# A 2 by 2 block scheme with seven block products for the gate and up products of a streaming encoder's feed-forward network

## The reference, cut to what matters

```
x = x + token_mix(rmsnorm(x, norm_mix), ...)          # attention, pooling, latent attention, convolution
h = rmsnorm(x, norm_ffn)                              # 640 tokens x 1024
x = x + (silu(h @ w_ff_gate) * (h @ w_ff_up)) @ w_ff_down
y = rmsnorm(x, norm_final)                            # after the second layer
```

## Time and profile before

| what | value |
|---|---|
| median of 3 runs | 2607.0 us (2605.19, 2607.0, 2620.18) |
| profiled execution | 2600.69 us, span 2598.9 us |
| TensorE busy, matmuls | 2454.0 us (94%), 15714 |
| mean granted TensorE clock | 0.969 of full |
| VectorE busy | 1063.2 us (41%) |
| ScalarE busy | 567.0 us (22%) |
| GpSimd busy | 1189.8 us (46%) |
| DMA | 186.01 MB, mean 72 GB/s |

### The profile page before, as it was taken

One profiled execution on the slowest core, in us unless ns is written; L12 is line 12 of the kernel. 1 busy time (PEld: TensorE's weight loads), 2 busy tenths in 40 slices (PEclk: granted clock), 3 DMA queues, 4 the chain that ended last, 5 costly groups with the idle time before them and its releaser, 6 DMA issues.

```text
span 2598.9 us, 44801 instructions
## 1 busy us (share of the span) xinstructions
PE 2454.0 (94%) x15714; PEld 2302.1 (89%) x15714; DVE 1063.2 (41%) x1940; ACT 567.0 (22%) x1080; POOL 1189.8 (46%) x1364
## 2 busy tenths in 40 slices
PE   6997999999999999999899889999999999999996
PEld 5996997777899999999899789977778999999996
DVE  6976253333236331232379643433322363303323
ACT  2014233333312210010111232323332121100100
POOL 3542554222366555655445335522214665555552
PEclk9998998999999999999899999989987999999998
DMA  5341121001132222222324312201001322222222
GB/s 170 126 120 33 62 67 52 29 25 37 37 123 74 75 66 73 84 78 67 122 70 134 92 45 70 65 25 37 25 25 49 122 74 73 69 78 81 73 65 73
DMA packets 73084, 186.01 MB, mean 72 GB/s; under 512 B 20381, under 2 KB 23549, under 8 KB 71934
## 3 DMA queue, kind: packets, MB, share of 16 engines
q1 hardware_dynamic: 55230, 161.54, 19.7%
q10 hardware_dynamic: 17728, 22.78, 2.7%
HBM read 171.72 MB, written 14.14 MB: 72 GB/s over the span
## 4 chain that ended last, share of the span: by engine, by line
PE 88%; DVE 4%; issue 3%; ACT 2%; ACTq 2%; DMA 1%; SPq 0%; DVEq 0%
PE gemm L466 75%; PE side L705 1%; PE side L723 1%; PE side L691 1%; PE side L707 1%; DVE rstd L1210 1%; PE side L708 1%; PE side L699 1%; PE side L715 1%; DVE h_lo L1215 1%; PE side L677 1%; PE side L609 1%; DVE softmax_stats L1476 0%; ACTq L1054 0%; ACT square L1098 0%
## 5 line engine op out<-in xcount | busy, mean ns | idle before, releaser
L431 POOL CAST w_hi<-w_raw 128x384 fp32r<-128x384 f32 (+3 forms) x680 | 397.2, 584 | 1320.9 <-PE gemm L466 1294.9
L433 POOL TENSOR_TENSOR w_lo<-w_raw,w_hi 128x384 fp32r<-128x384 f32 (+3 forms) x680 | 795.7, 1170 | 54.4
L466 PE MATMUL gemm<-h_hi,w_hi 128*128 128x320 f32 x3136 | 737.6, 317 | 21.7 <-DVE h_lo L1215 15.7
L466 PE MATMUL gemm<-h_lo,w_hi 128*128 128x320 f32 x3136 | 719.4, 311 | 0.0
L466 PE MATMUL gemm<-h_hi,w_lo 128*128 128x320 f32 x3136 | 718.9, 311 | 0.0
L466 PEld LDWEIGHTS gemm<-h_hi,w_hi 128*128 128x128 f32 x3136 | 525.4, 189 | 41.2 <-issue 33.7
L466 PEld LDWEIGHTS gemm<-h_lo,w_hi 128*128 128x128 f32 x3136 | 528.9, 189 | 0.0
L466 PEld LDWEIGHTS gemm<-h_hi,w_lo 128*128 128x128 f32 x3136 | 528.8, 189 | 0.0
L1292 DVE SCALAR_TENSOR_TENSOR side<-conv_prompt,vec,side 128x512 f32<-128x512 f32 x232 | 173.5, 748 | 0.0
L1534 DVE TENSOR_TENSOR x<-gemm,x 128x320 f32<-128x320 f32 x96 | 42.6, 486 | 302.3 <-PE gemm L466 302.3
L466 PE MATMUL gemm<-f_lo,w_hi 128*128 128x320 f32 x704 | 160.5, 309 | 0.0
(11 more groups left out here) (222 smaller groups left out, 2673.1 us busy)
## 6 DMA issues: line engine op xcount, KB each, us to landing
w_raw<-in_ws_gate SPq DMA_DIRECT2D x64, 512.0 KB, 3.4
w_raw<-in_ws_in SPq DMA_DIRECT2D x44, 512.0 KB, 3.4
w_raw<-in_ws_fg SPq DMA_DIRECT2D x44, 512.0 KB, 3.3
w_raw<-in_ws_fu SPq DMA_DIRECT2D x44, 512.0 KB, 3.3
w_raw<-in_ws_proj SPq DMA_DIRECT2D x64, 256.0 KB, 2.6
w_raw<-in_ws_d SPq DMA_DIRECT2D x32, 384.0 KB, 3.0
w_raw<-in_ws_d SPq DMA_DIRECT2D x32, 320.0 KB, 2.8
w_raw<-in_ws_out SPq DMA_DIRECT2D x16, 512.0 KB, 3.3
```

What stands on the lines that cost most here:

```text
L431: eng.tensor_copy(w_hi[s][:, cols], w_raw[s][:, cols]).then_inc(w_high.sem, 1)
L433: eng.tensor_tensor(w_lo[s][:, cols], w_raw[s][:, cols], w_hi[s][:, cols].bitcast(F32), ALU.subtract).then_inc(w_split.sem, 1)
L466: mm = eng.matmul(dst[:, hf, 0:HALF], w, r[:, k, cols], start=first and k == 0 and part == 0, stop=last and k == kk - 1 and part == 2)
```

## The change

**Seven products.** The gate tiles j and j+1, as a 1024 x 256 block of weights against 640 tokens, are seen as a 2 by 2 by 2 block product: weight blocks b11, b12 (first 4 weight tiles of tile j and of j+1) and b21, b22 (the last 4), activation blocks by token half and by half of the 1024 features. Plainly this is 8 block products of 12 matmuls (4 weight tiles, 3 parts, 320 tokens). The new code forms four sums of weights (T1 to T4) and four of activations (S1 to S4) and needs seven block products. One such group of seven is a *quad*; gate and up have one each per pair of tiles, 10 pairs and so 20 quads per layer. The first pair (tiles 0 and 1) stays plain: 4 units.

**Where it accumulates.** The five regions QX, QV (G[0]), QY, QW (G[1]) and QZ (bank 6) are 128x320. ACT copies a finished product from one region into the next one, where a later product is added on top, and into u2 and u4 in SBUF; DVE makes the last two sums.

**Activation blocks.** They need `rstd` inside, so DVE makes them after the norm: `act_block` (4 instructions of 128x320), `act_sum` (128x1280), ACT rounds with `act_high`, DVE `act_low`, once per layer, beside units 0 to 3 (listed at `gate_out(0)`). h_hi and h_lo are overwritten by them; the plain h of the feed-forward half is hu_hi, hu_lo.

**Weights.** Four raw buffers of 128x1024, and a ring of 5 hi/lo operands of 128x512. ACT now does all rounding (`cast`), POOL subtracts for plain operands, DVE for the sums of weights (`sum_low`) and makes the sums themselves (`weight_sums`).

**Chunks** are now 8, 8 and 6 tiles, so down units have 8, 8 and 6 weight tiles, 8 units in each chunk. **Both layers and all feed-forward tiles are written out** in Python instead of `Fori`. SP loads the small mixing weights of the second layer only after the last feed-forward product of the first, since the ring lies over them.

The diff, cut to its core (blank lines left out):

```diff
-K6, K5 = 6, 5
 CUT = 3
 UW = DM
+HW = UW // 2
+RING = 5
 BIG = float(2.0 ** 100)
 
...
+    def quad():
+        a = len(loads)
+        b = a + 1
+        quads.append(len(ops))
+        add(a, 0, HW)
+        first = plain
+        add(b, 1, HW, F_SUM3)
+        add(a, 0, HW, F_SUM2)
+        add(b, 0, HW)
+        add(a, 1, HW, F_SUM1)
+        loads.append((UW, first, sums))
+        add(b, 0, HW, F_SUM4)
+        add(b, 1, HW)
+        loads.append((UW, plain, sums))
...
         m_lo, o = sb("m_lo", [P, KT, T], F32R, o)
 
...
+        hu_hi, o = sb("hu_hi", [P, KT, T], F32R, o)
+        hu_lo, o = sb("hu_lo", [P, KT, T], F32R, o)
+        assert o == m_at
+        ah, al, af = [None] * 7, [None] * 7, [None] * 7
+        for n in range(4, 7):
+            ah[n], o = sb(f"act_hi{n}", [P, 4, HALF], F32R, o)
+            af[n], _ = sb(f"act{n}", [P, 4, HALF], F32, o)
...
+        f_lo01, o = sb("f_lo", [P, 2, T], F32R, o)
...
 
         relb, _ = sb("rel_bias_sb", [NBUCKET, NH], F32, R)
         hot, _ = sb("bucket_hot", [NBUCKET, RELW], F32, R + 64)
         relv, _ = sb("rel_values", [NH, RELW], F32, R + 64 + RELW * 4)
 
         G = [ctx.enter_context(nc.psum_tensor(f"gemm{s}", [P, 2, 512], F32)) for s in range(2)]
+        QX, QV, QY, QW = G[0][:, 0, 0:HALF], G[0][:, 1, 0:HALF], G[1][:, 0, 0:HALF], G[1][:, 1, 0:HALF]
...
+                for r, (width, _, _) in enumerate(FF_LOADS):
+                    if r < 2:
+                        eng.wait_ge(w_split.sem, w_split.at(l, 2 * UNITS - 2 + 2 * r))
+                    elif r < 4:
+                        eng.wait_ge(unit_done.sem, unit_done.at(l, UNITS - 1))
+                    else:
+                        _, plain, sums = FF_LOADS[r - 4]
+                        eng.wait_ge(lo_plain.sem, lo_plain.at(l, plain))
+                        if sums:
+                            eng.wait_ge(lo_sum.sem, lo_sum.at(l, sums))
+                    src = layer_of(io["ws_ff"], l * FF_STREAM + r) if r < FF_STREAM \
+                        else layer_of(io["ws_fd"], l * KT + (r - FF_STREAM))
+                    eng.dma_start(raw[r % 4][:, 0:width], src).then_inc(ff_loaded[r % 4].sem, 16)
 
             eng.wait_ge(outs.sem, outs.at(L, 0))
...
-                    pairs(p0, FC, UW, UW)
-                    pairs(p0 + FC, KT, K6 * P, K5 * P)
+                for n, op in enumerate(FF_OPS):
+                    if op.summed is None:
+                        src, hi, lo = ff_operand(n)
+                        eng.wait_ge(op_high.sem, op_high.at(l, n + 1))
+                        eng.tensor_tensor(lo, src, hi.bitcast(F32), ALU.subtract).then_inc(lo_plain.sem, 1)
 
 
...
+                def block_product(n, dst, act, fresh):
+                    _, wh, wl = weights(n)
+                    for k in range(4):
+                        cut = slice(k * P, (k + 1) * P)
+                        for t, (w, r) in enumerate(((wh, ah), (wh, al), (wl, ah))):
+                            mm = eng.matmul(dst, w[:, cut], r[act][:, k, :], start=fresh and k == 0 and t == 0,
+                                            stop=k == 3 and t == 2, skip_group_check=not fresh)
+                    mm.then_inc(op_done.sem, 1)
...
+                            eng.wait_ge(n_split.sem, n_split.at(l, i + 1))
+                        return i
+                    if units:
+                        psum(0, FF_G0 + units // 2)
+                    elif up:
+                        eng.wait_ge(gate_act.sem, gate_act.at(l, 4 * pair + 1))
+                    else:
+                        eng.wait_ge(up_first.sem, up_first.at(l, pair))
+                    block_product(n, QX, act(A11), True)
+                    if units:
+                        psum(1, FF_G0 + units // 2)
+                    else:
+                        eng.wait_ge(p_sum.sem, p_sum.at(l, 2 * q - 1))
+                    block_product(n + 1, QW, act(S3), True)
+                    eng.wait_ge(p_copy.sem, p_copy.at(l, 5 * q + 1))
+                    block_product(n + 2, QY, act(S2), False)
+                    block_product(n + 3, QX, act(A12), False)
+                    eng.wait_ge(p_copy.sem, p_copy.at(l, 5 * q + 3))
+                    block_product(n + 4, QV, act(S1), False)
+                    block_product(n + 5, QZ, act(A22), False)
+                    eng.wait_ge(p_copy.sem, p_copy.at(l, 5 * q + 5))
+                    block_product(n + 6, QV, act(S4), False)
...
+                eng.matmul(QZ, hu_hi[:, 0, 0:P], hu_hi[:, 0, 0:HALF], start=True, stop=True)
+                for u in range(1, 4):
+                    ff_unit(u, hu_tile)
+                u = 4
+                for c, size in enumerate(FF_CHUNKS):
...
+                def cast(n):
+                    op = FF_OPS[n]
+                    if n >= RING:
+                        eng.wait_ge(op_done.sem, op_done.at(l, n - RING + 1))
+                    if op.summed is None:
+                        eng.wait_ge(ff_loaded[op.load % 4].sem, ff_loaded[op.load % 4].at(l, 16 * (op.load // 4 + 1)))
+                    else:
+                        q = max(k for k in range(N_QUADS) if FF_QUADS[k] <= n)
+                        eng.wait_ge(t_made.sem, t_made.at(l, 4 * q + op.summed + 1))
+                    src, hi, _ = ff_operand(n)
+                    eng.activation(hi, src, ACT.Copy).then_inc(op_high.sem, 1)
...
...
+                cast(6)
+                cast(7)
+                silu(0)
+                cast(8)
+                act_high(A11, 4)
+                cast(9)
+                f_high(0, t2[1][:, :], 0)
+                act_high(S3, 9)
+                cast(10)
+                silu(1)
+                cast(11)
+                act_high(S2, 15)
+                act_high(A12, 19)
+                act_high(S1, 14)
+                act_high(A22, 13)
+                act_high(S4, 20)
+                cast(12)
...
+                    done(0)
+                    if units:
+                        eng.wait_ge(g_free[1].sem, g_free[1].at(l, 2 * (FF_G0 + units // 2)))
+                    copied(QX, QY)
+                    cast(n + 5)
+                    if q == 0:
+                        f_high(1, t2[1][:, :], 1)
+                    done(1)
+                    if q:
+                        eng.wait_ge(p_sum.sem, p_sum.at(l, 2 * q))
+                    copied(QW, QZ)
+                    cast(n + 6)
+                    done(2)
+                    if not up and q:
+                        eng.wait_ge(ff_value.sem, ff_value.at(l, 2 * pair))
+                    copied(QY, QV)
+                    copied(QY, u2)
+                    cast(n + 7)
+                    done(3)
+                    if not up:
+                        silu_block(QX, gb[0][:, lo_half])
...
+                    done(6)
+                    if not up:
+                        silu_block(QV, gb[1][:, lo_half])
+                        eng.wait_ge(p_sum.sem, p_sum.at(l, 2 * q + 2))
+                        silu_block(gb[0][:, hi_half], gb[0][:, hi_half])
+                    cast(n + 11)
+                    if up:
+                        for t in range(2):
+                            f_high(2 * pair + t, fb[t][:, :], f_index(pair) + t)
+                u = 4
+                for c in range(len(FF_CHUNKS)):
+                    for pair in ff_pairs(c):
...
+                    n = FF_QUADS[q]
+                    a, b = raw[FF_OPS[n].load % 4], raw[FF_OPS[n + 3].load % 4]
+                    b11, b12, b21, b22 = a[:, 0:HW], a[:, HW:UW], b[:, 0:HW], b[:, HW:UW]
+                    t1, t2_, t3, t4 = b12, t_sum[F_SUM2][:, :], t_sum[F_SUM3][:, :], t_sum[F_SUM4][:, :]
...
+                        made(2)
+                        split_before(5)
+                        eng.tensor_tensor(t4, b21, t2_, ALU.subtract).then_inc(t_made.sem, 1)
+                        return
+                    for k in (0, 3):
+                        load = FF_OPS[n + k].load
+                        eng.wait_ge(ff_loaded[load % 4].sem, ff_loaded[load % 4].at(l, 16 * (load // 4 + 1)))
+                    split_before(1)
+                    eng.tensor_tensor(t3, b22, b12, ALU.subtract).then_inc(t_made.sem, 1)
+                    made(1)
+                    split_before(2)
+                    eng.tensor_tensor(t2_, t3, b11, ALU.add).then_inc(t_made.sem, 1)
+                    made(2)
+                    eng.tensor_tensor(t1, b12, b11, ALU.subtract).then_inc(t_made.sem, 1)
...
+                def sum_low(n):
+                    src, hi, lo = ff_operand(n)
+                    eng.wait_ge(op_high.sem, op_high.at(l, n + 1))
+                    eng.tensor_tensor(lo, src, hi.bitcast(F32), ALU.subtract).then_inc(lo_sum.sem, 1)
...
+                def act_block(dst, k0, cols):
+                    for k in range(4):
+                        eng.scalar_tensor_tensor(dst[:, k, :], x[:, k0 + k, cols],
+                                                 vec[:, V_GFFN + k0 + k:V_GFFN + k0 + k + 1], rstd[:, cols],
```

(64 more changed lines are left out.)

370 lines of the change are left out of this document (280 added, 90 removed).

## The result

The changed kernel took 2529.2 us (median of 4 runs, 2520.8 to 2539.9), the kernel before 2610.3 beside it (4 runs, 2605.2 to 2620.2): ratio 0.9687, 95% interval 0.963 to 0.9744. It is faster by 81 us. Forecast were 25, and 2529 lies outside the range of 2555 to 2625.

The account below looks back on a forecast made before the run. The prediction took TensorE's number of matmuls, 146.7 ns apart, to bound the feed-forward halves. Its terms, -70.4 + 5 + 36 + 5 = -24.4 us, gave 2582 us against the median 2607, range 2555 to 2625.

Parts of the forecast that it names:

- loops written out: Layer and feed-forward loops written out in Python: no gain, 0 us, with bounds -2.3 and 0.
- Removed work: Gate and up products: 240 fewer matmuls per layer, 480 in all, at 146.7 ns each, -70.4 us.
- Steady quads: Quads after the entry: sixth operand 0.3 us late in 14 gate quads, +5 us (0 to 14).
- The exclusion: VectorE work on two SBUF inputs and GpSimd subtractions exclude each other: 24.1 of 24.64 us per pair of quads.
- rival B: VectorE and GpSimd together bound every quad, first at gate quads' sixth operand: 58 us more, 2640 us; chance 0.16.
- The entry: Start of each feed-forward half: TensorE waits for VectorE's operands, first quad 16.7 us late plus 1.3 for clock; +36 us.
- Into the down units: First down unit after quads waits for VectorE's read of G[0], six times: +5 us (3.5 to 7).
- Loads: Weight loads, two per quad with four buffers, and the later small mixing weights of layer two: cost nothing.
- twelve matmuls in one bank: Twelve matmuls in a row onto one bank instead of alternating between two: taken as zero; 7 ns each would cost 24 us.
- Rival A: Feed-forward entry mostly covered, steady quads clean: -70.4 + 25 + 0 + 3.5 = -42, 2565 us; chance 0.24.
- the forecast case: Whole kernel: the summed terms, -24.4 us, landing at 2572 to 2595 us; chance 0.45.
- Rival C: Branches were dear: 21 loop-backs per layer at 1 us each on the path, -42 more, 2540 us; chance 0.03.

Follow-up runs that it names:

- the run with four more instructions: Changed kernel with four more VectorE maxima of a 128x512 constant spread over each of the 17 quads per layer that prepare a next one: 2564.0 us.
- the reordered one: Changed kernel with VectorE's and ScalarE's instruction order at the feed-forward entry rearranged: 2532.2 us; with half-length filler matmuls through the sample attention 2519.0 us.

## Why the prediction was wrong, step by step

**The failed step is "loops written out: 0 (bounds -2.3 and 0)".** Measured alone, they are worth 50 us between the medians. It rested on two readings. The gapless 3120 matmuls showed that the loops cost nothing in the feed-forward half, which is right (463.5 against 464.0), but the change also wrote out the loops around the mixing half, where TensorE does wait, and no row of its latent heads was read. And the 2.25 us of issue before ScalarE's table load were taken for all that a table load can cost. There the load ran beside TensorE's norm sums (from 1286.82 for 2.50 us) and was free; in every latent head it stands behind the later of two waits, on the path, 1.2 us each. Of the 19.1 us that the heads gave, 12 distances of 1.19 make 14.3. The rest, 4.3, is the first distance of the second layer (30.3 to 26.0), and it is not the loops' own: it follows the length of the half clock in the first head, in kernels of either kind.

**The second part of the failed step is the clock**, for whose change in the mixing half the prediction had no term. In the kernel before, beside all experiments, 1 of 76 runs had no stretch at half clock, 15 had one, 60 two. Of the changed kernel and the five variants with its mixing half and no filler (35 runs), 23 had none. At 17 to 20 us each that is 17 us in the profiled pair and, with 1.8 and 0.35 stretches a run, about 26 between the experiments' runs; with the heads' 19 it makes up most of the 50. It also explains the two groups of the changed kernel's runs. Shown is that what TensorE does within the sample attention decides: filled all through, the long stretch is gone in 10 of 10 runs of the kernel before (1 of 76 without filler) and in 6 of 6 of the reordered one (2 of 6 without). Not shown is why writing out any engine's loops makes it rarer. Each group of engines did part, and so did the early Exp with the loops kept; the rival that any shift in the timing of the side work does it, and not the loops as such, stays open. Within one execution of the same code one layer has it and the other not, so a single profile says little about it. The Trainium skill (TensorE: Matmul & The Clock Gate, What's actually happening) says that the gate follows how busy TensorE was of late and that its watch is not tied to the kernel's start. The fillers agree with the first (no long stretch in 16 runs); the second would let two layers of one execution differ, as 205.3 and 222.3 us do in the profiled execution of before, but no run here isolates it.

**Removed work**: right. 480 matmuls, 146.7 ns from one to the next before and in the quads, -70.4.

**Steady quads, +5**: measured 0. One pair of quads in the changed kernel:

```profile
1005.52:1030.17 24.65, 24.65 (x171) 24.65 (x170) 19.60 (x27) 14.78 (x30) 8.28 (x7) 1.00 0.27 86
```

VectorE 19.6 and GpSimd 8.3, with stretched instructions counted as busy: VectorE has 5 us free, not 0.5. The exclusion itself was seen again, VectorE at 1035.30 beside GpSimd at 1034.77:

```profile
1035.30 1.78 DVE L1915 TENSOR_TENSOR ring_lo<-w_sum,ring_hi 128x512 fp32r<-128x512 f32 x1
```

```profile
1034.77 1.76 POOL L598 TENSOR_TENSOR ring_lo<-w_raw,ring_hi 128x512 fp32r<-128x512 f32 x1 [4.26 <-ACT ring_hi L1401]
```

0.68 us of work end 0.55 after GpSimd. That is the sixth operand: done at 1037.08, 6.9 us into its quad (forecast 9.1, wanted at 8.8), because one such turn fell ahead of it and not two. Of GpSimd's 8.3 us per pair only some 3.3 (an estimate, 19.6 less the 16.3 of plain work in the prediction) stretched VectorE's. That work with an input in PSUM is not slowed, the prediction read from an overlap of 0.10 us, which shows little; it holds, for 30 such instructions of 128x320 began inside a GpSimd subtraction here and took 0.48 us, as outside one. So the exclusion was right and adding its time in full was wrong; the run with four more instructions shows where rival B begins.

**The entry, +36**: the mechanism right, the size 28.2. TensorE in the entry of the changed kernel, ahead of products one, two and five of the first layer and five and six of the second:

```profile
840.39 0.61 PE L989 MATMUL gemm<-act_hi,ring_hi 128*128 128x320 f32 x1 [4.96 <-issue]
844.09 0.61 PE L989 MATMUL gemm<-act_hi,ring_hi 128*128 128x320 f32 x1 [0.17 <-DVE ring_lo L1915]
854.47 0.38 PE L989 MATMUL gemm<-act_hi,ring_hi 128*128 128x320 f32 x1 [4.51 <-DVE ring_lo L1915]
2091.69 0.39 PE L989 MATMUL gemm<-act_hi,ring_hi 128*128 128x320 f32 x1 [2.50 <-DVE ring_lo L1915]
2096.28 0.39 PE L989 MATMUL side<-act_hi,ring_hi 128*128 128x320 f32 x1 [2.59 <-DVE ring_lo L1915]
```

It stood 4.96 us ahead of product one (forecast 6.2). The first quad ends with product seven, 859.76 + 1.76 = 861.5; without a wait it would have been 835.4 + 12.32 = 847.7. That is 13.8 late in the first layer, and 14.4 in the second (second quad's product six at 2110.36, less 8.80, against 2074.80 + 12.32), where 16.7 + 1.3 were forecast. From the first remainder's end to the sixth operand VectorE took 16.8 us and not 18.1; the reciprocal started 0.54 after ScalarE, not held up by the weight sums. The operand waited for is one earlier than forecast: in the first layer the fifth, behind five remainders of activations, after which the sixth came just in time; in the second layer the fifth and the sixth. The half clock after the stand is there too: product five of the first layer, 12 matmuls, took 3.01 us and not 1.76.

**Into the down units, +5**: 1.20, 1.20 and 0.70 per layer, 6.2 in all. **Loads and twelve matmuls in one bank, 0**: right, 10.56 us for 72.

Together -70.4 + 28.2 + 6.2 = -36.0, against -37.4 measured in the feed-forward halves and -24.4 forecast; the 1.4 between are not followed up. Rival A (-42) was nearer than the forecast case. Rival C had the sum (2540 against 2529) by luck and with the wrong reason: it priced each loop-back at 1 us, but nearly all of them are in the feed-forward halves, where 3120 matmuls ran without a gap, and the 50 us came with the layer loops, which go back once per engine. The rule of the Trainium skill on instruction fetch (Runtime: NRT & Kernel Launch, Instruction fetch mechanics), cited in the prediction, pointed the right way; that a fetch was on the path, no run here shows.
